# Cross attention reordered, and three waits or placements changed on the way to it, in a one-layer decoder kernel on one core

## The reference

```python
h = rms_norm(x, norm_mix)
(mq, mk, mv, mo, mi, mf, aq, ak, av, gu, gv, gate_pre) = split(h @ w_in, SPLIT_POINTS)
merged = g0 * (mlstm(...) @ w_a) + g1 * (dilated_attention(...) @ w_b) + g2 * (spatial_gating(...) @ w_c)
x = x + merged @ w_out

# cross attention, 4 heads of 128, 256 memory tokens
q = rms_norm((rms_norm(x, norm_xattn) @ w_xq).reshape(b_, s_, 4, 128), qk_g[0])
k, v = split(rms_norm(mem, norm_mem) @ w_xkv, 2)
k = rms_norm(k.reshape(b_, m_, 4, 128), qk_g[1])
logits = einsum('bshd,bmhd->bhsm', q, k) * 128 ** -0.5
p = softmax(logits)
x = x + einsum('bhsm,bmhd->bshd', p, v).reshape(b_, s_, 512) @ w_xo

x = x + grouped_moe(rms_norm(x, norm_ffn), router, experts)   # 16 experts, top 2
```

## Time and profile before

| | |
|---|---|
| time, median of 3 runs | 685.05 us (680.68 to 687.97) |
| profiled execution | 679.54 us, of which the profile's span is 677.7 us |
| TensorE busy with matmuls | 95% of the span |
| VectorE, ScalarE busy | 74%, 64% |
| the chain that ended last | TensorE 71%, VectorE 13%, issue 8%, ScalarE 5% |
| granted TensorE clock, mean | 0.99 |
| DMA | 164 MB, 242 GB/s over the span |

### The profile page before, as it was taken

The page is one execution under the profiler, slowest core; times in us unless marked ns, Lnnn a source line. Parts: engine busy times, 40 slices in busy tenths (PEclk is TensorE's granted clock), DMA queues, the critical chain, the costliest instruction groups (busy, mean ns, idle before and its releaser), DMA issues.

```text
span 677.7 us, 8736 instructions
## 1 busy us (share of the span) xinstructions
PE 646.5 (95%) x3026; PEld 511.0 (75%) x3026; DVE 500.4 (74%) x568; ACT 435.5 (64%) x476; POOL 19.2 (3%) x13
## 2 busy tenths in 40 slices
PE   5999999999999999999989899999999999999996
PEld 4887888778777788888877777767677777687774
DVE  4543696753775539867655769998899889989996
ACT  6544637434945447354564758789877897788781
POOL 0100000400100000000000000000000000000000
PEclk9999999999999999999999789999999999999999
DMA  9945466643533255555049238999799979998961
GB/s 339 362 164 181 163 239 226 242 161 116 196 93 94 106 205 187 188 186 186 1 135 423 98 115 292 384 391 359 301 386 376 377 277 370 386 381 319 364 252 62
DMA packets 49053, 164.04 MB, mean 242 GB/s; under 512 B 4377, under 2 KB 9179, under 8 KB 36732
## 3 DMA queue, kind: packets, MB, share of 16 engines
q1 hardware_dynamic: 44432, 158.81, 63.3%
q10 hardware_dynamic: 4588, 4.80, 2.2%
HBM read 162.53 MB, written 2.64 MB: 244 GB/s over the span
## 4 chain that ended last, share of the span: by engine, by line
PE 71%; DVE 13%; issue 8%; ACT 5%; DVEq 2%; DMA 1%; SPq 0%; ACTq 0%
PE ps L1481 14%; PE ps L1473 14%; PE ps L1474 14%; PE ps L1854 8%; DVE w_lo L1229 6%; PE ps L1454 4%; PE ps L1899 3%; PE ps L1884 3%; PE ps L1836 2%; PE ps L1641 1%; DVEq L1395 1%; PE ps L1616 1%; DVE y_lo L1373 1%; ACT w_hi L762 1%; PE ps L1857 1%
## 5 line engine op out<-in xcount | busy, mean ns | idle before, releaser
L903 DVE TENSOR_TENSOR w_lo<-w_raw,w_hi 128x2048 fp32r<-128x2048 f32 (+2 forms) x54 | 118.5, 2211 | 56.2 <-ACT w_hi L501 55.6
L1473 PE MATMUL ps<-w_hi,act_hi 128*128 128x512 f32 (+1 forms) x304 | 118.6, 392 | 1.7 <-ACT w_hi L501 1.7
L501 ACT ACTIVATE w_hi<-w_raw 128x2048 fp32r<-128x2048 f32 (+2 forms) x54 | 99.1, 1855 | 27.4 <-PE ps L1481 26.1
L1474 PE MATMUL ps<-w_hi,act_lo 128*128 128x512 f32 (+1 forms) x304 | 116.3, 384 | 0.0
L1229 DVE TENSOR_TENSOR w_lo<-w_raw,w_hi 128x2048 fp32r<-128x2048 f32 (+1 forms) x48 | 99.4, 2108 | 6.8 <-ACT w_hi L762 6.0
L1229 DVE TENSOR_TENSOR w_lo<-e_raw,w_hi 128x2048 fp32r<-128x2048 f32 (+2 forms) x48 | 97.3, 2064 | 1.4 <-ACT w_hi L762 1.3
L762 ACT ACTIVATE w_hi<-w_raw 128x2048 fp32r<-128x2048 f32 (+1 forms) x48 | 83.8, 1765 | 0.2 <-issue 0.2
L762 ACT ACTIVATE w_hi<-e_raw 128x2048 fp32r<-128x2048 f32 (+2 forms) x48 | 82.2, 1728 | 1.1 <-PE ps L1854 1.0
L1854 PE MATMUL ps<-w_hi,xg 128*128 128x512 f32 x236 | 75.0, 436 | 1.0 <-DVE xg L1366 1.0
L1481 PE MATMUL ps<-w_lo,act_hi 128*128 128x512 f32 (+1 forms) x304 | 74.4, 387 | 0.0
L1473 PEld LDWEIGHTS ps<-w_hi,act_hi 128*128 128x128 f32 x304 | 57.1, 188 | 14.3 <-issue 3.3
(11 more groups left out here) (316 smaller groups left out, 959.8 us busy)
## 6 DMA issues: line engine op xcount, KB each, us to landing
w_raw<-in_w_in SPq DMA_DIRECT2D x32, 1024.0 KB, 5.4
w_raw<-in_w_expert_gate SPq DMA_DIRECT2D x24, 1024.0 KB, 7.1
e_raw<-in_w_expert_down SPq DMA_DIRECT2D x24, 1024.0 KB, 7.8
w_raw<-in_w_expert_up SPq DMA_DIRECT2D x16, 1024.0 KB, 8.3
e_raw<-in_w_expert_up SPq DMA_DIRECT2D x16, 1024.0 KB, 7.2
e_raw<-in_w_expert_gate SPq DMA_DIRECT2D x8, 1024.0 KB, 9.4
w_raw<-in_w_expert_down SPq DMA_DIRECT2D x8, 1024.0 KB, 7.0
w_raw<-in_w_xkv SPq DMA_DIRECT2D x4, 1024.0 KB, 5.8
```

The source lines that it names most:

```text
L501: A(bview(w_hi, b, blocks[b].shape), bview(w_raw, b, blocks[b].shape), ACT.Copy).then_inc(hi_done, 1)
L903: V.tensor_tensor(bview(w_lo, b, sh), bview(w_raw, b, sh), f32(bview(w_hi, b, sh)), ALU.subtract).then_inc(lo_done, 1)
L1473: MM(o, xh[:, t0 + k, i * P:(i + 1) * P], wh[:, k], start=first and k == 0, stop=False)
L1474: MM(o, xl[:, t0 + k, i * P:(i + 1) * P], wh[:, k], start=False, stop=False)
```

## The change

It does five things.

- The logits of both tiles are issued at once, ahead of the values' hi products for tile 1 and of their lo products.
- VectorE's order becomes maxima 0, 1, 2, normalise 0, maxima 3, normalise 1, 2, 3; after that VectorE takes the values out of PSUM (chunk `C_V1` goes from `by_act` to `by_dve`).
- The wait for the moved values goes from ahead of the turns of the probabilities to ahead of the products, and these wait by head pair: heads 0 and 1 for three of the copies to `xpT`, heads 2 and 3 for the fourth.
- The lo products of block 27 are parted from its hi products and follow the last turns of queries and keys; `gate_third(0)` goes ahead of `attn_scores(1)`.
- The turn of the gates waits for one copy to `pre` (the one that empties bank 4) where it waited for all four.

```diff
-        by_act = [c for c in range(C_B)] + [C_K, C_V1]
+        by_act = [c for c in range(C_B)] + [C_K]
...
             for v in range(2 * NT):
-                if v == 2:
-                    move(C_V1, *[(xkv[:, i, XW:2 * XW], acc(C_V1, i), ACT.Copy, rs_mem[:, i:i + 1]) for i in range(NT)])
                 act.wait_ge(s["x_max_done"], v + 1)
...
-            for t in range(NT):
-                x_maxima(2 * t)
-                x_maxima(2 * t + 1)
-                x_normalise(2 * t)
-                x_normalise(2 * t + 1)
+            for v in range(3):
+                x_maxima(v)
+            x_normalise(0)
+            x_maxima(3)
+            for v in range(1, 2 * NT):
+                x_normalise(v)
+            dve.wait_ge(mm_done, first_block[C_V1 + 1])
+            for i in range(NT):
+                ins = V.tensor_scalar(xkv[:, i, XW:2 * XW], acc(C_V1, i), rs_mem[:, i:i + 1], None, ALU.mult)
+            ins.then_inc(ev_dve, 1)
...
-            pe.wait_ge(s["conv_in_ready"], 4)
+            pe.wait_ge(s["conv_in_ready"], 1)
...
                 if n == 4:
-                    in_block(27, act_hi, act_lo)
+                    in_block(27, act_hi, act_lo, part="hi")
...
+            in_block(27, act_hi, act_lo, part="lo")
             pe.wait_ge(s["aqk_moved"], 6)
...
+                if u == 0:
+                    gate_third(mine.pop(0))
                 if u < 7:
                     attn_scores(u + 1)
...
-            values_block("hi", range(1, 2))
             pe.wait_ge(s["xk_moved"], 2)
...
-                if t == 0:
-                    values_block("lo")
-            pe.wait_ge(*moved(C_V1))
+            values_block("hi", range(1, 2))
+            values_block("lo")
...
-            pe.wait_ge(s["x_probs_moved"], 2 * NT)
+            pe.wait_ge(*moved(C_V1))
             for h in range(XH):
+                if h % 2 == 0:
+                    pe.wait_ge(s["x_probs_moved"], NT + h // 2 + 1)
```

## The result

The changed kernel takes 675.63 us (median of 4, 674.84 to 676.89) where the kernel before, on the same chip, takes 682.87 us (median of 4, 679.14 to 687.97). Three executions in the experiments further down, of 924, 2224 and 3583 us, were disturbed: the medians given there hold them, the ratios and the counts of executions don't.

A forecast was written before the change was run, and what follows sets the result against it. The prediction took TensorE, holding 71% of the chain of waits, to bound the kernel. Gates 1.5, attention's two edits 0 each and cross attention 1.9 summed to 3.4 us off 685.05, giving 681.6 us, range 676.7 to 686.3.

The forecast's parts named there:

- Gates' wait, 1.5 us: At the gates' turn: waiting for the first copy to `pre` only removes TensorE's 1.54 us wait; taken as 1.5 us.
- Block 27 parted and the third first, 0: At attention's opening: VectorE is late, so neither edit gains; TensorE waits about 1.2 us instead of 0.47; price 0.
- The wait for `qkT`: Before attention: TensorE's 0.9 us wait for last copies of queries and keys would be covered by lo products; price 0.
- Cross attention, 1.9 us: In cross attention: reordering and VectorE's move of the values start the products at 354.85 instead of 356.78; gain 1.9 us.
- the finer wait: Cross attention's wait by head pair: gives nothing, since its first half also waits for the values.
- The queue behind it: SyncE's expert loads behind cross attention: issued at 351.8, 1.7 us later, hidden within seven us of room.
- The gather: Ahead of the experts: 6.85 us of gather matmuls at half speed cost at most 3.4 us more than at full.
- the clock's better side: Ahead of the experts: clock returns before the gather, giving up to 3.4 us more, 678.2 us; chance 0.10.
- the clock in cross attention: In cross attention: clock stays at 1.00 through 346 to 361 us, with TensorE idle for less than before.
- nothing in the change acts on what made them differ: Whole kernel: the median's 5.5 us above the profiled execution and the 7.3 us spread were left unaffected by the change.
- The signs of being wrong: Products later than 354.5, attention opening at the same time, or the stretch from the gather on differing over 1 us.

The follow-up runs named there:

- e1: The kernel before with only the gates' turn waiting for one copy to `pre` instead of four: 682.00 us, ratio 0.9965.
- e2: The kernel before with only the two attention edits, block 27 parted and `gate_third(0)` first: 683.49 us, ratio 1.0001.
- e13: The changed kernel without the two attention edits (block 27 parted, `gate_third(0)` first): 677.30 us, ratio to the kernel before 0.9888.
- e16: The changed kernel, unchanged, measured a third time: 676.94 us, ratio to the kernel before 0.9894.
- e8: The changed kernel with 21 unused matmuls in TensorE's gaps in router and gather: 676.13 us, ratio to the kernel before 0.9895.
- e4: The kernel before, unchanged, timed once more as if it were a change: 685.04 us, ratio 1.0016.
- e7: The kernel before with all of cross attention's edits except issuing both tiles' logits first: 681.97 us, ratio 0.9963.
- e5: The kernel before with eight unused matmuls between the turns of tile 0 and tile 1 in cross attention: 680.41 us, ratio 0.9944.
- e9: The changed kernel, unchanged, measured again: 676.88 us, ratio to the kernel before 0.9896.
- e6: The kernel before with only the values moved by VectorE and the waits that go with it: 683.14 us, ratio 0.9993.
- e11: The kernel before with the gates' finer wait and eight unused matmuls among cross attention's turns: 679.51 us, ratio 0.9954.
- e15: The changed kernel without the attention edits, ScalarE moving tile 0's values and VectorE tile 1's: 677.16 us, ratio to the kernel before 0.9896.

## Why the prediction was wrong

*Gates' wait, 1.5 us:* right. 1.46 in the profile, the turn at 65.8. e1's medians differ by 2.9, more than the profile's gain; six of its twelve executions have the higher clock (0.989), where the kernel before beside it had four of 29. Why a wait at 65 us changes how often the clock falls at 355 was not tried.

*Block 27 parted and the third first, 0:* right in amount (e2 1.0001, and e13 against e16), and the wait came as told, 1.40 us for the 1.2 forecast. The wait for `qkT`, which the lo products were to cover, went from 0.9 to 0.6 and not to nothing; the path doesn't lie there.

*Cross attention, 1.9 us:* right on the path, 2.03. Each step stands: the maximum waits for GpSimd, the exponentials run with no gap over 0.1 us, VectorE is the late engine, the move and the fourth copy end within 0.02 us of each other, the finer wait gives next to nothing. The products start 3.5 us earlier with the start's 1.8 taken off, for 3.4 forecast.

*The queue behind it:* right in what counts, since ScalarE's first split, at 359.34, has no wait. The expert loads went out 0.7 later than forecast: the text reads 0.7 us from the products' end to the issue and then leaves it out (351.8, next to products that end at 351.7). By the earlier trace rows that distance is 0.49 us, and it is the same after.

*The gather:* the clock's better side, to which I gave a chance of 0.10, came in small: 0.3 to 0.9 us in the profiles. Its price of up to 3.4 us was too high. With the clock at 1.00 in e8 the gather's matmuls ran from 386.52 to 392.93, 6.4 us, where before they ran from 388.62 to 396.36, 7.7 us: halving the busy time of TensorE took no account of the copies.

*The step that failed* is the clock in cross attention. The text said that there "the clock stays at 1.00 through 346 to 361 with TensorE idle for 3.0 of 15 us; it will be idle for less", and of the 5.5 us between the profiled execution and the median that "nothing in the change acts on what made them differ". The first was true of one execution in eight, as far as the mean clocks tell. The second followed from it and was false: what made them differ was, for 4.1 us, a fall of the clock in the very stretch that the change shortens. The trace was there for a better reading. A median 5.5 us above the profiled execution at the same code asks for a mechanism. And TensorE's list of waits, of which the text says that two entries lie in the change, has a third there, longer than both:

```profile
PE ps L1454 <- DVE xp L1215: 2.2, 2, 1.8
```

It is idle time among turns, and the earlier trace rows show a fall ahead of the experts, where TensorE is idle in pieces too. I looked for the clock's risk only where the one trace already had it. The signs of being wrong that the text names stayed away for the same reason: they look at the path of one execution, and there the forecast held. A term of 4.1 us times the share of executions that fall, in place of zero, would have given 678. That could not be sized from one trace; that the term was put at nothing without a reason could be seen.

The sum of the parts as the runs have it: against an execution without the fall 1.46 + 2.03 = 3.5 us, and 0.3 to 0.9 at the gather; against the usual one 4.1 us more, 7.9 to 8.5 in all, for 8.2 between the medians (684.9 and 676.7). The first measurement's before had, by their times, two executions of each kind among its four (679.14 and 680.68, 685.05 and 687.97); their clocks are not on record. That puts its median between the groups, and the distance at 7.2.

## What to carry to other kernels

When the profiled execution is far below the median of the same code, the profile may lack the main effect: look for stretches where TensorE turns small blocks and idles, and price a halved clock behind them before saying that the spread is noise. Such a stretch is cheaply tested by filling it with unused matmuls; if the time falls though nothing starts sooner, the clock was the price. And a reordering that puts large products into such a stretch can be worth more by what it does for the clock than by the wait it takes away.

## What the runs showed of the hardware that was not expected

- The same program fell into two groups on each of four chips (mean clocks 0.978 to 0.987 in 93 of 106 executions, 0.990 and 0.991 in 13), at 4.1 us between the medians. Where a profile shows the fall, the clock went to half speed among the turns and idle times of 1.0 to 1.8 us (e2, e4, e7) or only when the products behind them had begun (e1, 358.9 us).
- In e4's profile 2.25 us were lost in cross attention and 1.85 behind it, 1.64 of these in sixteen router products that ran at half speed (3.61 us for 1.97).
- The first hi products of an execution ran at 0.63 us each, 0.43 apart, in twelve of eighteen profiles (the kernel after, e4, e5, e9 and others) and 0.39 in the other six (the kernel before, e2, e6, e11, e15, e16), while the granted clock of these stretches reads 1.00; this shifts everything behind it by 1.3 to 2.9 us and is no part of any edit. The column doesn't show such a start; the durations do.
- VectorE moved two 128x512 tiles out of PSUM in 1.41 us, ScalarE in 1.27; where both engines meet, as here, a split between them brought the products 0.4 us forward and no measurable time.
